# Seven-product slabs in the up-projections, with the weight sums of the first three layers on GpSimd

## The reference, cut to what matters

```
def conv_ffn(h, w_up, conv_w, conv_b, w_down):     # four times, FF_DIM = 2816
    a = h @ w_up                                   # 256 x 1024 by 1024 x 5632
    pad = jnp.pad(a, ((0, 0), (CONV_W - 1, 0), (0, 0)))
    y = conv_b
    for j in range(CONV_W):                        # three taps along the tokens
        y = y + conv_w[j] * pad[:, j:j + S, :]
    gate, val = jnp.split(y, 2, axis=-1)
    return (jax.nn.silu(gate) * val) @ w_down
```

## Time and profile before

| | us |
|---|---|
| median of 3 runs | 2855.99 (2854.76 to 2856.97) |
| profiled execution, own time | 2856.74 |
| its span | 2854.0 |
| busy: PE, DVE, ACT, POOL | 2775.2, 1186.7, 423.4, 93.3 |

### The profile page before, as it was taken

How to read it: one execution, slowest core, us unless ns; L and a number is a source line. 1 busy time by engine, 2 the same in 40 slices (tenths; PEclk the granted TensorE clock), 3 DMA queues, 4 the chain that set the end, 5 groups by cost and what they waited for, 6 DMA issues and landing times.

```text
span 2854.0 us, 48197 instructions
## 1 busy us (share of the span) xinstructions
PE 2775.2 (97%) x20796; PEld 2145.6 (75%) x20796; DVE 1186.7 (42%) x2649; ACT 423.4 (15%) x862; POOL 93.3 (3%) x180
## 2 busy tenths in 40 slices
PE   8999999999999999999999999999999999998987
PEld 7888898889898889888898888988436324742634
DVE  4556774677464676213356720556410111010011
ACT  2112203220223220211211200021000100100000
POOL 0111100110000110000000000000000000000000
PEclk9999999999999999999999999999999999999999
DMA  9778843886424885434444344444999999999996
GB/s 361 281 284 295 301 168 117 291 299 222 160 101 168 301 304 197 148 133 148 157 164 149 118 149 158 160 152 189 373 426 425 426 427 426 412 426 427 425 427 263
DMA packets 96874, 753.40 MB, mean 264 GB/s; under 512 B 10416, under 2 KB 11952, under 8 KB 41520
## 3 DMA queue, kind: packets, MB, share of 16 engines
q1 hardware_dynamic: 71344, 658.37, 59.4%
q0 software_dynamic: 25344, 92.29, 9.4%
HBM read 749.57 MB, written 1.05 MB: 263 GB/s over the span
## 4 chain that ended last, share of the span: by engine, by line
PE 85%; DMA 10%; DVE 4%; ACT 1%; issue 0%; SPq 0%; DVEq 0%; ACTq 0%
PE ps L653 28%; PE ps L1371 11%; PE ps L759 8%; PE ps L1401 6%; PE ps L730 4%; PE ps L1116 4%; PE ps L773 3%; DMA UW<-w_moe_up 3%; PE ps L883 3%; PE ps L683 2%; DMA UW<-w_moe_down 2%; PE ps L791 2%; PE ps L1241 2%; DMA HT<-w_moe_up 2%; PE ps L1039 2%; DMA B<-w_moe_up 2%
## 5 line engine op out<-in xcount | busy, mean ns | idle before, releaser
L653 PE MATMUL ps<-HT,ring 128*128 128x256 f32 x3840 | 831.4, 379 | 0.0
L653 PEld LDWEIGHTS ps<-HT,ring 128*128 128x128 f32 x3840 | 729.0, 190 | 99.6 <-issue 1.0
L2217 DVE SCALAR_TENSOR_TENSOR C<-ps,vec,C 128x255 f32<-128x255 f32 (+1 forms) x336 | 146.5, 477 | 173.4 <-ACT C L1560 170.4
L2081 DVE SCALAR_TENSOR_TENSOR B<-B,cact 128x1024 f32<-128x1024 f32 x160 | 188.7, 1219 | 7.7 <-DMA B<-w_ada 7.7
L2770 DVE TENSOR_TENSOR C<-C,ps 128x256 f32<-128x256 f32 (+1 forms) x80 | 30.8, 387 | 369.9 <-ACT C L1819 369.9
L1116 PE MATMUL ps<-HT,ring 128*128 128x256 f32 x640 | 143.8, 380 | 0.0
L1116 PEld LDWEIGHTS ps<-HT,ring 128*128 128x128 f32 x640 | 120.2, 190 | 16.8 <-issue 1.2
L1560 ACT ACTIVATE C<-ps,vec 128x256 f32<-128x256 f32 x168 | 85.8, 560 | 287.8 <-PE ps L653 285.2
L1371 PE MATMUL ps<-B 128*32 128x512 f32 (+1 forms) x1216 | 122.1, 554 | 5.9 <-DMA B<-w_moe_up 5.9
L2787 DVE TENSOR_TENSOR X<-X,ps 128x512 f32<-128x512 f32 x24 | 16.5, 687 | 241.2 <-PE ps L1332 240.7
L730 PE MATMUL ps<-A,ring 128*128 128x256 f32 x512 | 110.8, 379 | 0.0
(11 more groups left out here) (504 smaller groups left out, 3512.8 us busy)
## 6 DMA issues: line engine op xcount, KB each, us to landing
ring<-w_ff_up SPq DMA_DIRECT2D x88, 1024.0 KB, 7.6
B<-w_ada POOLq DMA_DIRECT2D x144, 512.0 KB, 7.7
B<-w_moe_up SPq DMA_DIRECT2D x32, 2048.0 KB, 24.6
ring<-w_moe_up SPq DMA_DIRECT2D x32, 2048.0 KB, 25.4
ring<-w_ff_down SPq DMA_DIRECT2D x36, 1024.0 KB, 5.0
A<-w_moe_up SPq DMA_DIRECT2D x16, 2048.0 KB, 24.9
HT<-w_moe_up SPq DMA_DIRECT2D x16, 2048.0 KB, 26.2
UW<-w_moe_up SPq DMA_DIRECT2D x16, 2048.0 KB, 25.2
```

The source lines that it names most:

```text
L653: last = mm(bank[:, j * n:(j + 1) * n], ring[:, slot, k * 256 + j * P:k * 256 + j * P + P], src[:, k, :], start=(k == 0), stop=(k == KD - 1))
L2081: return stt(out=w, in0=w, scalar=1.0, in1=cact[:, :], op0=ALU.mult, op1=ALU.mult, accum_out=mod[:, n:n + 1])
L2217: ins = stt(out=o, in0=src[:, half * TOK:(half + 1) * TOK - d], scalar=vec[:, c + 2 - d:c + 3 - d], in1=o, op0=ALU.mult, op1=ALU.add)
```

## The change

- `UP_SEVENS` names the slabs of each up-projection that are multiplied by seven products: 4, 6, ... 18 in layers 0 to 2 (eight each), 3 to 18 in layer 3, 3 to 21 in the SwiGLU. Those slabs are laid out on the host by blocks. They use two banks each, from four pairs in turn.
- The sums of values of the input H are made by VectorE behind slab 1 (`up_value_sums`).
- The sums of weights of slab m+2 are made by VectorE in step m in layer 3 and the SwiGLU (`up_weight_sums`), and by GpSimd in layers 0 to 2, inside its loop over the DMAs of the modulation tiles: those for slab m stand before the DMA of tile 2m+4.
- VectorE puts a seven slab together first (`up_together`), into SBUF; ScalarE and VectorE take the taps from there.
- MLA: the swapped halves are no longer multiplied; ScalarE makes them by copies of 32 rows (`halves_swapped`). `mla_a` has two slabs, `mla_qb` six banks. VectorE computes the scales before it turns q.
- Experts' loop: the last slot of a round is loaded and used in two halves; the two units' rows lie in two banks, one copied by ScalarE, the other by VectorE; the squares are made by ScalarE; a Sqrt is placed ahead of the rows.
- Loops over slabs are written out on ScalarE, VectorE and TensorE for these sections. In the down-projections the banks change, and the second half of `seven_s` moves.

```
+UP_SEVENS = {("sw_up", 0): range(3, KF), ("ff_up", DEPTH - 1): range(3, 19)}
+for layer in range(DEPTH - 1):
+    UP_SEVENS["ff_up", layer] = range(4, 20, 2)
+POOL_SUMS = [f"ff_up{layer}" for layer in range(DEPTH - 1)]
+UP_PAIRS = [(2, 3), (4, 7), (5, 6), (0, 1)]
...
         @block.gpsimd
+            def sums_of_weights(g, sums):
+                pool.wait_ge(slab_done, g - 1)
+                pool.wait_ge(w_ready[g % RING], 16 * (g // RING))
+                w = seven_w(g)
+                tt(sums[:, 2], w[:, 0], w[:, 2], ALU.subtract)
+                step(tt(sums[:, 0], w[:, 2], w[:, 3], ALU.add))
+                step(tt(sums[:, 1], sums[:, 0], w[:, 0], ALU.subtract))
+                tt(sums[:, 3], w[:, 1], sums[:, 1], ALU.subtract).then_inc(pool_summed.tick(), 1)
...
                 for n in range(ADA_TILES):
+                    m = n // 2 - 2
+                    if n % 2 == 0 and m in UP_SEVENS["ff_up", i]:
+                        sums_of_weights(first_slab["ff_up", i] + m, up_s[m % 2])
                     q = ADA_LATE + i * ADA_TILES + n
                     if n >= ADA_DEEP:
                         pool.wait_ge(ada_used, ADA_FIRST + q - ADA_DEEP + 1)
...
         @block.tensor
+            def sevens(g, banks, sums, values, summed, lo, hi, count, wait_values, summer=weights_summed):
+                x, y = ps[banks[0]], ps[banks[1]]
+                w = seven_w(g)
...
+                    if n == 2 and wait_values:
+                        values_summed.wait(pe)
+                    elif n == 3:
+                        summer.wait(pe)
...
+            def gemm_up(sec):
+                g0 = first_slab[sec]
+                for t in range(1, KF):
+                    g, bank = g0 + t, up_banks(t)[0]
+                    slab_wait(g)
+                    bank_wait(sec, t)
+                    if t in UP_SEVENS[sec]:
+                        sevens(g, up_banks(t), up_s[t % 2], H4, up_t, 0, KD // 2, KD // 2, t == UP_SEVENS[sec][0],
+                               pool_summed if sec[0] + str(sec[1]) in POOL_SUMS else weights_summed)
...
         @block.vector, ffn
                 for m in range(KF):
+                    if m in UP_SEVENS[sec]:
+                        up_together(sec, m, up_out[m % 2][:, 0:TOK], up_out[m % 2][:, TOK:2 * TOK])
+                    up_value_sums(sec, m)
+                    up_weight_sums(sec, m + 2)
                     one(m)
                     if i + 1 < DEPTH and 0 < m < KF - 1:
                         ada_next(n + 2 * m - 2)
...
+            def up_together(sec, m, first, second):
+                dve.wait_ge(slab_done, first_slab[sec] + m + 1)
+                together(up_banks(m), first, second, S[:, :, :].rearrange("p a t -> p (a t)")).then_inc(put_together.tick(), 1)
+                put_together.own(dve)
+                nc.vector.memset(small[:, 44:45], 0.0).then_inc(free_dve, 1)
...
         @block.scalar, mla
+                def halves_swapped(dst, src):
+                    for n in range(4):
+                        lo, other = n * ROPE // 2, (n ^ 1) * ROPE // 2
+                        ins = af(dst[lo:lo + ROPE // 2, :], src[other:other + ROPE // 2, :], ACT.Copy)
+                    return ins
...
         @block.sync, last slot of a round of the experts' loop
+                        sp.dma_start(slot_of[b][:, 0:SLOT // 2], src[:, 0:SLOT // 2]).then_inc(half_ready, 16)
+                        sp.dma_start(slot_of[b][:, SLOT // 2:SLOT], src[:, SLOT // 2:SLOT]).then_inc(moe_ready[b], 16)
```

More of the change, by code:

```diff
@@ L744, in gemm_seven @@
                         slab_wait(g)
[L745 to L761, removed]
+                        if m == 0:
+                            part_wait(lo, hi)
+                        sevens(g, UP_PAIRS[m], seven_s[(3 * m + part) % 2], A4, seven_t, lo, hi, PAIRS, m == 0)
+            def gemm_up(sec):
[7 more added lines that the diff above has]
+                               pool_summed if sec[0] + str(sec[1]) in POOL_SUMS else weights_summed)
+                    elif t == 1:
+                        pair_as_made(ps[bank], g % RING).then_inc(slab_done, 1)
+                    else:
+                        pair(ps[bank], g % RING, H).then_inc(slab_done, 1)
             def gemm_last(sec, src, before_banks):
@@ L1392, in down @@
                     for q in range(DOWN_SLOTS):
-                        slot_ready(r, n)
+                        halves = loop and q == DOWN_SLOTS - 1
+                        if not halves:
+                            slot_ready(r, n)
                         slot = slot_of[n % BUFFERS]
@@ L1825, in rows @@
                     dst = y_slot[0 if loop else flip_of[batch_of[r]]]
+                    if loop:
+                        af(small[:, 47:48], eps[:, 0:1], ACT.Sqrt)
                     act.wait_ge(moe_used, slots_before(r, "down") + DOWN_SLOTS)
                     for g in range(4):
[L1828 removed]
+                        for u in range(1 if loop else nu):
                             ins = af(dst[(at + u) * UNIT:(at + u + 1) * UNIT, g * TOK:(g + 1) * TOK],
@@ L1938, in two, with up_value_sums, together, halves @@
+            def up_value_sums(sec, m):
+                if m == 1 and UP_SEVENS[sec]:
+                    dve.wait_ge(slab_done, first_slab[sec] + 2)
+                    sums_of_values(H4, up_t)
+            def together(banks, first, second, scratch):
+                x, y = ps[banks[0]], ps[banks[1]]
+                one, u, uu = scratch[:, 0:P], scratch[:, P:TOK], scratch[:, TOK:2 * TOK]
                 def two(ap):
                     return ap.rearrange("p (o t) -> p o t", o=1).to_broadcast([P, 2, P])
+                def halves(ap):
+                    return ap.rearrange("p (o t) -> p o t", o=2)
@@ L2868, in deep, with sevened @@
     return w.reshape(parts, tiles, P, 8, P).transpose(3, 0, 2, 1, 4).reshape(8 * parts, P, tiles * P)
+def sevened(slabs, which):
+    slabs = slabs.copy()
+    for m in which:
+        slabs[m] = slabs[m].reshape(P, KD // 2, 2, 2, P).transpose(0, 3, 2, 1, 4).reshape(P, SLAB_TILES * P)
+    return slabs
 def in_sevens(w):
```

335 lines of the change are left out of this document (195 added, 140 removed).

## The result

The changed kernel takes 2992.89 us (median of 4 runs, 2992.69 to 2993.08) against 2855.84 (2854.76 to 2856.97) for the one before: ratio 1.0479, 95% interval 1.0464 to 1.0494. That is 137 us slower. The forecast was 2944, the range 2888 to 2990: the side and the place were right, the size was 49 us too small, just outside the range. The profiled execution has a span of 2990.7 us, 136.7 over that of before.

The account below looks back on a forecast made before the run. TensorE, busy 97% of the span, was taken to bound the kernel; 104.4 + 3.2 - 10.3 - 6.9 - 2.7 = +87.7 us on the median of 2855.99 gave 2943.7, range 2888 to 2990.

Parts of the forecast that it names:

- the main term: Layers 0 to 2: TensorE waits for GpSimd's sums of weights, made behind the modulation-tile refills; 104.4 us lost in all.
- two slabs take 8.45 + 0.83 + P + 0.1 + 3.57 = 12.95 + P: Layers 0 to 2, a seven-product and a plain slab: second tile's end, gap, sums, release, products behind the wait; before 13.83 us.
- P: GpSimd's time for the four sums of weights of a slab in layers 0 to 2: 5.5 us, ends 2.7 and 9.8.
- The engines also exclude each other: Rival, layers 0 to 2: VectorE's and GpSimd's two-input SBUF operations wait each other out; +31 us, 2975, chance 0.29.
- The sum of layers 0 to 2: Each layer loses 8P - 9.2 = 34.8 us, three lose 104.4 (ends 37 and 208).
- Layer 3: VectorE, also making weight sums, needs 7.4 us a slab, over TensorE's 6.25: +3.2 us (ends -10.6 and +10).
- MLA: 32 TensorE records go, ScalarE makes twelve copies of 32 rows in exchange: -6.9 us (ends -8 and -1).
- SwiGLU: 19 slabs gain 12.6 us, the down-projection's late first weight sums give 2.3 back: -10.3 us (ends -12.6 and -6).
- Experts: Loop waiting for DMA: last slot in two halves, copies split with VectorE, squares on ScalarE: -2.7 us (ends -5 and +2).
- The other VectorE work fits: Layers 0 to 2: step m+1 is done at 13.5 of the 18.45 us period; 2.65 us value sums fall in the wait.
- follow each other without a gap: TensorE's down-projections: already unrolled, seven products without gaps, so written-out instructions instead of loops were given 0 us.
- The rival that would not be slower: Layers 0 to 2: sums reached in time, P hidden, VectorE sets 13.5 us a pair; -25.7 us, 2830, chance 0.08.

Follow-up runs that it names:

- e2: Changed kernel with GpSimd's sums of weights in layers 0 to 2 moved two refills forward in its order: 2883.62 us.
- e1: Changed kernel with 23 unread 128-column products on TensorE ahead of its wait for GpSimd's last sum in layers 0 to 2: 2970.61 us.
- e6: Changed kernel with one of GpSimd's four sums of weights made and three left out in layers 0 to 2: 2869.74 us, one run.
- e8: Changed kernel with the sums of weights in layers 0 to 2 left out, zeros put and waited for once a layer: 2835.13 us, one run.
- e4: Changed kernel with VectorE in place of GpSimd making the sums of weights in layers 0 to 2: 2871.03 us.
- e3: Changed kernel with plain slabs only in layers 0 to 2, the rest of the change kept: 2840.30 us.
- e10: Order of e2, with three GpSimd fills of the whole 128x2048 tile in place of its four sums: 2834.35 us, one run.

## Why the prediction was wrong, step by step

- **Where the loss is** (the main term): right. The wait comes before the fourth product of each even slab, for GpSimd's last sum, and e2 shows that it hangs on the sums' place behind the refills. Slab's end to the end of the second tile 8.34 us (said 8.45), gap to the sums 0.84 (0.83), release of TensorE 0.05 (0.1), wait 5.59 (5.3).
- **The step that failed**: the last term of "two slabs take 8.45 + 0.83 + P + 0.1 + 3.57 = 12.95 + P". The 3.57 us behind the wait were read from rows of an engine that had not stood still. After 5.3 to 5.6 us of idle time they are 5.13 to 5.38, at a granted clock of 0.50. That is 1.56 to 1.81 more in each of 21 periods, 35 us, and 1.7 at the first wait of layers 1 and 2, 3 us. e1 takes most of it away, and the waits of 0.76 us in e6 have none of it. No rival of mine had it.
- **P**, the second term that was mis-sized: 6.11 us in 15 slabs, 5.84 in six and 5.25 in three, for 5.5, so +10 us in all. The sums by themselves were a little shorter than I said (5.25), and the rest is the turns that they wait for, 0.86 and 0.59 us. "The engines also exclude each other" stood as a rival at 0.29 with +31, from 1.3 us in each of 24 slabs. The turns are real, and they cost 16 us on this path; the others fall on VectorE, which stood idle later anyway: its sums of values in step 8 take 7.2 us for 2.65, and the wait hides them. The rival's 2975 lies nearer to the measured time than my forecast, but the exclusion alone does not explain it.
- **The sum of layers 0 to 2**: the other terms were each a little early (0.15 in 21 periods, -3). 35 + 3 + 10 - 3 = 45 of the 45.9 us that these layers lost beyond the 104.4 (150.3).
- The Trainium skill, "SBUF — State Buffer", "Who interferes with whom", has the exclusion as a lock between a VectorE instruction with two inputs in SBUF and a GpSimd instruction that reads SBUF, and leaves out those with one input there and those beside a GpSimd instruction that only writes. The trace agrees in all three: a tile beside sums takes 2.28 us for 1.22, the taps with an input in PSUM stay at 1.77, and taps from SBUF beside fills at 1.79. "GPSIMD Engine Reference", "Performance versus the Vector engine", has GpSimd's two-input fp32 sum at 1.96 times VectorE's, at 2048 elements a partition: for 128x512 here it is 1.26 to 1.33 for 0.69, 1.83 to 1.93. My 1.22, put together from two rows of other work, was the worse number for one instruction; the 0.30 that I added twice for the waits between them brought the four sums back to 5.5, over the 5.25 measured.
- **Layer 3**: +3.4 for +3.2, period 7.36 for 7.4. **MLA**: -6.9, as said. **SwiGLU**: -8.4 for -10.3; the wait at the down-projection is 2.11 (said 2.3), and 1.7 more go to the slow clock behind it, the same step again. **Experts**: -1.5 for -2.7. "The other VectorE work fits": true in the changed kernel, where the waits hide it; without the waits it just fits the up-projection with no GpSimd beside it (e8), and doesn't with GpSimd's sums (e2). That the seven products of the down-projection "follow each other without a gap" was read from its first slab; the second one waits 0.58 us, before and after alike.
- **The rival that would not be slower** (the sums reached in time, 2830): e2 is that case, and gives 2884. Its "P stays hidden" held up to slab 8, its 13.5 us for VectorE left the turns out (15.07).

## What to carry to other kernels

A wait of several microseconds on TensorE can be charged twice, once as idle time and once in the products behind it (here all 21 waits of 5.3 to 5.6 us were), so a forecast must not take those products from rows where the engine was busy. Work placed on an idle engine stands in that engine's queue and, where both read SBUF, in the neighbour's time as well: look first at what is queued ahead of it, then at what runs beside it. And where an engine is near its limit for the stretch, a smaller share of the new work (here none, or one slab in three) is worth more than all of it.

## What the runs showed of the hardware

- The slow clock after an idle time does not go by the length of the wait alone. Behind the same wait of 3.50 us in layer 3 the 24 records took 2.94 us in the changed kernel, 4.57 in e4 and 5.49 in e3. In the changed kernel a wait of 2.78 us (layer 0) left the clock alone, and those of 2.69 (layers 1 and 2) did not. Nor did waits of 1.97 (e8, at the down-projection) and 1.95 (e1, slab 12, behind 5.3 us of filling). All 21 waits of 5.3 to 5.6 us showed it.
- GpSimd fills 128x2048 fp32 in 1.8 us without slowing VectorE (e10: taps 1.79, tiles 1.22); the same engine's sums of 128x512 take turns with VectorE's two-input work (tiles 2.28, four taps from SBUF 3.86).
